# Moving the stationary operands of a two-block transformer kernel by 32 bytes in on-chip memory

## The reference

```python
x = first_block(x, mem, ...)    # retention + forgetting attention, cross attention over 256 rows, SwiGLU (2816)
return second_block(x, c, ...)  # SwiGLU, conv + sliding-window attention, gated merge, SwiGLU, final rms_norm

# first_block
hn = rmsnorm(h, g_mix[l]);  proj = hn @ w_in[l]
h = h + jnp.concatenate([ret, fox], axis=-1) @ w_out[l]
h = h + memory_cross_attention(rmsnorm(h, g_xattn[l]), mem, w_xq[l], w_xkv[l], g_mem[l], g_xq[l], g_xk[l], w_xo[l])
hn = rmsnorm(h, g_ffn[l])
h = h + (jax.nn.silu(hn @ w_gate[l]) * (hn @ w_up[l])) @ w_down[l]

# second_block, three parts of this kind, each with a shift, a scale and a gate from c
h = modulate(rms_norm(x, g_ffn1[l]), sh1, sc1)
x = x + 0.5 * gt1[:, None, :] * swiglu(h, w1_gu[l], w1_down[l])
```

## Time and profile before

| | before |
|---|---|
| median of 3 runs (lowest to highest) | 2006.04 us (2005.62 to 2006.31) |
| span of the profiled execution | 2004.3 us; the page gives no other time of its own for it |
| PE busy, matmuls | 1982.4 us (99%), 11,622 |
| PEld busy | 1717.1 us (86%) |
| DVE, ACT, POOL busy | 1236.5, 898.6, 905.8 us (62%, 45%, 45%) |
| DMA engines busy | 36% of the span |
| granted TensorE clock | 0.998 of full speed |

### The profile page before, as it was taken

One profiled execution on the slowest core, in us unless ns is written; L12 is line 12 of the kernel. 1 busy time (PEld: TensorE's weight loads), 2 busy tenths in 40 slices (PEclk: granted clock), 3 DMA queues, 4 the chain that ended last, 5 costly groups with the idle time before them and its releaser, 6 DMA issues.

```text
span 2004.3 us, 32457 instructions
## 1 busy us (share of the span) xinstructions
PE 1982.4 (99%) x11622; PEld 1717.1 (86%) x11622; DVE 1236.5 (62%) x1937; ACT 898.6 (45%) x1605; POOL 905.8 (45%) x458
## 2 busy tenths in 40 slices
PE   9999999999999999999999999999999999999998
PEld 7788788878999988899998888887777888999887
DVE  4675885346788787877768774463552247777111
ACT  4334444344566522556652252225663245666322
POOL 3344323326577655544445434443224445444443
PEclk9999999999999999999999999999999999999999
DMA  6243212212333286333338635322222223333321
GB/s 209 90 152 106 74 64 83 86 33 94 106 105 105 95 314 247 101 115 105 105 95 326 237 120 149 116 95 85 68 70 85 89 89 95 105 105 105 103 98 63
DMA packets 67246, 234.71 MB, mean 117 GB/s; under 512 B 7632, under 2 KB 9040, under 8 KB 66640
## 3 DMA queue, kind: packets, MB, share of 16 engines
q1 hardware_dynamic: 66432, 232.29, 35.3%
q10 hardware_dynamic: 720, 1.15, 0.2%
HBM read 225.54 MB, written 2.10 MB: 114 GB/s over the span
## 4 chain that ended last, share of the span: by engine, by line
PE 94%; DVE 3%; ACT 1%; issue 1%; DMA 0%; POOL 0%; SPq 0%; POOLq 0%; DVEq 0%; ACTq 0%
PE bank L2254 12%; PE bank L2255 12%; PE bank L2260 12%; PE bank L2433 9%; PE bank L2434 9%; PE bank L2437 9%; PE bank L2378 5%; PE bank L2379 5%; PE bank L2384 5%; PE bank L2228 1%; PE bank L2230 1%; PE bank L2229 1%; PE bank L2552 1%; PE bank L2560 1%; PE bank L2553 1%; PE bank L2870 1%
## 5 line engine op out<-in xcount | busy, mean ns | idle before, releaser
L538 POOL TENSOR_TENSOR wlo<-raw,whi 128x1024 fp32r<-128x1024 f32 x233 | 579.9, 2490 | 807.7 <-ACT whi L657 807.4
L657 ACT ACTIVATE whi<-raw 128x1024 fp32r<-128x1024 f32 x233 | 245.8, 1057 | 475.0 <-PE bank L2384 217.7
L2254 PE MATMUL bank<-xh,whi 128*128 128x512 f32 x764 | 302.0, 395 | 1.2 <-DVE xl L1355 0.9
L2255 PE MATMUL bank<-xl,whi 128*128 128x512 f32 x764 | 297.7, 390 | 0.0
L2378 PE MATMUL bank<-hh,whi 128*128 (+1 forms) x480 | 186.9, 389 | 1.0 <-ACT whi L657 1.0
L2379 PE MATMUL bank<-hl,whi 128*128 (+1 forms) x480 | 186.8, 389 | 0.0
L2260 PE MATMUL bank<-xh,wlo 128*128 128x512 f32 x736 | 181.6, 389 | 0.0
L2254 PEld LDWEIGHTS bank<-xh,whi 128*128 128x128 f32 x764 | 143.5, 188 | 34.9 <-issue 4.7
L2255 PEld LDWEIGHTS bank<-xl,whi 128*128 128x128 f32 x764 | 143.5, 188 | 29.5 <-issue 0.7
L2260 PEld LDWEIGHTS bank<-xh,wlo 128*128 128x128 f32 x736 | 138.1, 188 | 28.9
L2434 PE MATMUL bank<-xl,whi 128*128 128x256 f32 x648 | 162.5, 283 | 0.0
(11 more groups left out here) (396 smaller groups left out, 4510.0 us busy)
## 6 DMA issues: line engine op xcount, KB each, us to landing
raw<-units SPq DMA_DIRECT2D x341, 512.0 KB, 3.7
ada_w<-ada_rows SPq DMA_DIRECT2D x72, 512.0 KB, 5.6
h<-x_t SPq DMA_DIRECT2D x8, 256.0 KB, 5.3
out_t<-h SPq DMA_DIRECT2D x8, 256.0 KB, 2.1
raw<-units SPq DMA_DIRECT2D x4, 256.0 KB, 4.5
mem_in<-mem_t SPq DMA_DIRECT2D x1, 1024.0 KB, 11.2
turned_q<-proj SPq DMA_DIRECT2D x4, 256.0 KB, 5.1
dec<-decays SPq DMA_DIRECT2D x4, 256.0 KB, 4.7
```

The costliest lines, as they stand in the source:

```text
L538: pool.tensor_tensor(wlo[:, j % 2 * UNIT:(j % 2 + 1) * UNIT], raw[:, j * UNIT:(j + 1) * UNIT], whi[:, j % 2 * UNIT:(j % 2 + 1) * UNIT].bit ...
L657: act.activation(whi[:, v % 2 * UNIT:(v % 2 + 1) * UNIT], raw[:, slot * UNIT:(slot + 1) * UNIT], ACT.Copy).then_inc(hi_ready, 1)
L2254: mm(bank[:, 0:n], wh, chunk(rhs[0], t, n), start=t == 0, stop=False)
L2255: mm(bank[:, 0:n], wh, chunk(rhs[1], t, n), start=False, stop=False)
```

## The change

No instruction is added, removed or moved. The buffers `whi` and `wlo` begin 32 bytes later relative to a 64-byte line, by a filler of 8 fp32 ahead of them and one of 8 behind them. `w_t1`, `w_t2` and `w_t3_high` are placed 32 bytes later within their regions; a filler of 16 fp32 behind `ssum` and 16 more columns of `side` make room for that. `w_t3_low` stands at 32 bytes past a line before and after. New addresses: `whi` 67,744, `wlo` 75,936, `w_t2` 92,384, `w_t3_high` 96,480, `w_t1` 128,800, all 32 past a multiple of 64. `h`, `xh`, `xl` and `raw` stay; `tmp` and `xn` move by 64 bytes, `rstd` to `dec` by 128, `arena` (with `hh`, `hl`, `yh`, `memh` and the like) by 192, so these still begin on a multiple of 64.

```diff
-        raw, whi, wlo = sb("raw", 4 * UNIT), sb("whi", 2 * UNIT, f32r), sb("wlo", 2 * UNIT, f32r)
+        raw = sb("raw", 4 * UNIT)
+        sb("weights_lead", 8)
+        whi, wlo = sb("whi", 2 * UNIT, f32r), sb("wlo", 2 * UNIT, f32r)
+        sb("weights_trail", 8)
         tmp = sb("tmp", 4 * T)
         xn_at = nc.sbuf_base
         xn = sb("xn", 2 * T)
-        ssum, rstd = sb("ssum", T), sb("rstd", T)
+        ssum = sb("ssum", T)
+        sb("ssum_trail", 16)
+        rstd = sb("rstd", T)
...
-        side = sb("side", 12 * 256)
+        side = sb("side", 12 * 256 + 16)
...
-        side_at = arena_at - 12 * 1024
+        side_at = arena_at - 12 * 1024 - 64
+        half_line = 1 / 32
...
-        w_t1 = at("w_t1", 8, 8 * P, f32r, base=side_at)
-        w_t2 = at("w_t2", 0, 8 * P, f32r, base=xn_at)
-        w_t3_high = at("w_t3_high", 4, 4 * P, f32r, base=xn_at)
+        w_t1 = at("w_t1", 8 + half_line, 8 * P, f32r, base=side_at)
+        w_t2 = at("w_t2", half_line, 8 * P, f32r, base=xn_at)
+        w_t3_high = at("w_t3_high", 4 + half_line, 4 * P, f32r, base=xn_at)
```

## The result

The changed kernel takes 2032.12 us (median of 4 runs, 2031.77 to 2032.41), beside 2006.17 us for the kernel before in the same session. The ratio is 1.0132 with a 95% interval of 1.0118 to 1.0147: 1.3% slower. The forecast was 1.5% faster, and the time lies above the stated range.

What follows compares the result with a forecast made beforehand. The prediction took PE's matmul stream as the bound; gains of 15.5 and 17.2 us summed to 32.7, about 31 us on the chain, so 2006 - 31 = 1975 us, 1.5% less. The range was 1930 to 2010 us.

Steps and rivals of the forecast that it cites:

- The bound: Whole kernel: PE, busy 99% and 94% of the chain; time is matmul count times start-to-start distance, plus little.
- The remainder of 13.3 ns: Matmuls of 256 and 512 columns: about 13.3 ns each beyond their columns, read as an address-dependent collision of operand reads.
- First term: 256-column matmuls in fast products and memory layers: 3.3 ns gained on each of 4,704, 15.5 us.
- The sample: Four w_t3_low matmuls, already 32 bytes off a line: 0.46 us against 0.48, taken as 116.7 ns, 3.3 ns less each.
- Second term: 512-column matmuls with whi and wlo: 3.3 ns gained on each of 5,220, 17.2 us.
- the bound below zero: 512-column matmuls: if the offset kept streams at the just-broken 231.3 ns, 4.4 ns lost on 5,220, 23 us.
- Third and fourth terms: Writers and readers of moved buffers, and buffers moved by 64, 128 or 192 bytes: both taken as zero.
- The rules weighed against it: Skill rules on independent read ports and 16-byte SBUF lines: by both the change does nothing, 2006 us.
- the prediction's second rule: SBUF port swizzle: lines of 16 bytes, a shift by 32 keeps the place within one, so no effect.
- The slower one: Dense layers and down: 512 columns stay at 231.3 ns, 23 us lost against 15.5 gained, 2014 us; chance 0.13.

Runs made afterwards that it cites:

- e7: Kernel before with only w_t1, w_t2 and w_t3_high moved by 32 bytes, other operand distances kept modulo 256: 2.7 us faster.
- e6: Isolated matmul streams, none of the reference's work, stationary operand at 0 to 512 bytes, moving at 0 or 64; 512 columns: 226.9 ns at 256, 233.1 at 32.
- e5: Changed kernel with 64 bytes ahead of whi, none behind, and w_t1, w_t2, w_t3_high without their 32 bytes: slower than before by 0.8%.
- e1: Kernel before with every buffer, activations and weights alike, moved by 32 bytes: ratio 1.0003.
- e4: Isolated streams of 48 matmuls, none of the reference's work, stationary offset 0 to 128, moving 0 to 64 bytes: 226.7 ns at 32 and 32, 233.3 at 64 and 0.
- e10: Isolated 256-column products, none of the reference's work, alternating between distance 0 and another distance: 113.3 ns each at 192, 120 ns at 0.
- e9: Kernel before with w_t1, w_t2, w_t3_high, w_t3_low at a distance of 64 bytes, s4_hi and s4_lo moved by 192: 1998.86 us.
- e11: Kernel before with the w_t buffers 192 bytes (modulo 256) from their moving operands, s4_hi and s4_lo moved by 64: 2000.71 us.

## Why the prediction was wrong, step by step

**The bound.** Right. PE holds 94% of the chain before and after, nothing else moved, and the change of the time is the count of matmuls times the change of the time from start to start, to 0.1 us.

**The remainder of 13.3 ns.** Right in kind: it depends on the addresses. It was read as a cost that an offset from a 64-byte line removes; what counts is the distance of the two operands modulo 256 bytes. It is 13.4 ns at the good distance of 512 columns (226.7 - 213.3) and 20.5 ns in the row of the changed kernel (233.8 - 213.3). Before was already in the best of the eight positions for its 5,152 wide matmuls in streams, so no such shift could remove any of it.

**First term, 256 columns: 3.3 ns on 4,704, 15.5 us.** The sign was right and the size off: 1.51 ns on 4,953, 7.5 us. The sample did not stand for what the change does. `w_t3_low` was at a distance of 96 from `xh`, while the changed kernel has 32, 96, 160 and 224, and it was four matmuls between streams at 0. "The address is what differs" was too strong: e7 shows the sample at 120.4 ns with its distance as it was. In the changed kernel it went from 116.7 to 117.8 ns at the same place on its line, now at a distance of 32. That this term came out at half its size, and not at nothing, the sample had not shown.

**Second term, 512 columns: 3.3 ns gained on 5,220, 17.2 us.** This is the step that failed. The sign was carried over from the other width, because the remainder was equal. It measured +6.55 ns on 5,152 matmuls, a loss of 33.7 us; from 0 every other distance in steps of 32 costs 2 to 7.5 ns at this width, e6 says. (By the trace 5,259 matmuls have this width, not 5,220: 48 small ones were to be left out, not 90. That changes little.) The prediction called this its weakest step and gave the row that spoke against it, the weight load of 188 ns at 512 columns; the bound below zero, 4.4 ns from the earlier trace rows, was also too narrow. The mistake in the bound was to take the average of a transient for the worst that a stream can show.

**Third and fourth terms, nothing.** Right for the other engines: VectorE writes `w_t` in 684 ns, 683 before. Not quite for the arena: `hh` at 96 and not at 32 costs 1.0 ns on its matmuls (234.3 against 233.3).

**The rules weighed against it.** In e6, with no other engine at work, the same matmuls on `x_a` take 226.9 or 233.3 ns by the place of the weights alone. The shift by 32 bytes, which the prediction's second rule has without effect, costs 6.2 ns there (233.1). The Trainium skill, "TensorE: Matmul & The Clock Gate", section "Part 2: What happens when you issue a matmul", has the two reads on independent ports, so that the next weights take nothing from the running matmul; for fp32r these runs do not agree, since the time hangs on where the two operands stand to each other, and the measurement decides.

**The rivals.** The slower one, with a chance of 0.13, is the one that came true. It named the right place (the dense layers and `down` leave 226.9 ns and stay near 231) and the right point of decision: 3.0 ns at 512 columns. Its price was off on both sides, the loss too low and the gain too high: 23 - 15.5 = 7.5 us against 33.7 - 7.5 = 26.2. Its picture of a stream that stays unsettled fits the trace of e6, read start by start: at a distance of 64 the matmuls take 236 and 231 ns by turns to the last, while the last stream on `x_a,w_a` at 512 columns is at 226 or 227 ns after three. What in the reading of memory makes the difference, no run shows.

## What to carry to other kernels

When a stream of fp32r matmuls with 512 columns and a new weight tile each bounds the time, keep the stationary and the moving buffers a multiple of 256 bytes apart, both on 32 bytes: each other distance tried costs 2 to 7.5 ns a matmul, here up to 1.3% of the kernel. Any edit that adds or resizes a small buffer can lose that unnoticed, as the 64-byte step of e5 did. And a sample of one width says nothing of the sign at another. Here the kernel before had all its wide matmuls at the regular place, a distance of 0, which turned out the best; the forecast had given a loss 0.13.

## What the runs showed of the hardware

- The rhythm of a fp32r stream depends on the distance of the two operands modulo 256 bytes, with no other engine active. At 512 columns it is 226.7 ns at 0 and at 256, 229.1 at 192, 232.5 to 234.2 elsewhere. At 256 columns it is 120 ns at 0 and 160, 117 to 119 in most other places (e6). The runs give this dependence, not what makes it.
- The absolute place does not count in steps of 32 bytes (e1: ratio 1.0003), but does at 16: both operands at 16 show 233.1 ns, both at 32 226.7 (e4, one stream each).
- 256-column streams have a second rhythm of 113.3 ns, seen in isolation at distances of 192 (e4, e10) and nearly reached in kernels at 64, where isolated streams show 118: 114.6 ns in the mean of `xh` and `xl` with `whi` and `wlo` in e5, 115.6 for the `s4` buffers in e9. In e6 the distance of 192 ran at 117.9, in e11 at 117.7. What brings it about, and so whether a kernel can hold it, is not settled; it is worth up to 6.7 ns on each of some 4,500 matmuls here.
